# Prompt attention in a decoder layer: keys on the partitions, four heads at a time

## The chip, the cores and the metric

The kernel runs on one core of one Trainium2 chip. Its time is the device time of one execution in microseconds (us); three runs of the kernel before gave 2463.38, 2450.45 and 2455.8, median 2455.8. The profile is one more execution, recorded by the hardware profiler.

## The reference

One inference step of one decoder layer for a prompt of 1024 tokens and 8 sample sequences of 4 tokens (width 1024). A normalized input is projected to three mixers (sparse attention, a recurrent block, gated linear attention), whose outputs are merged and followed by an MLP. The change is in the sparse attention of the prompt, which has 8 heads of 64 in 2 groups (4 heads share a key/value head) and three branches for each head:

```python
# compressed: one key per 32 tokens; selected: all blocks here (16 of 16); window: the last 512 tokens
s = einsum(q, k) * 64 ** -0.5 + bias[bucket(pos_q - pos_k)]
s = where(mask, s, -inf)                     # causal; in the window also dist < 512
p = exp(s - max(s)) / max(sum(exp(s - max(s))), 1e-30)
o = g_cmp * (p_c @ v_c) + g_sel * (p_s @ v_s) + g_win * (p_w @ v_w)    # g: sigmoid gates per head
```

The bias depends on the distance alone and is constant from 128 tokens on; the constant part falls out of the softmax, so only the two nearest key tiles of 128 need a bias.

## The kernel before

All stages run one after the other; each is a block in which every engine has its own written-out program, and engines wait for each other by semaphores only. There is no planner: the order on an engine is the order of its program. Matrix products with weights are done as three f16 products (high by high, low by high, high by low parts); `Dense` (L360 to L434) streams weight tiles of 512 KB through four f32 buffers `w32`, and ScalarE and VectorE split each into f16 parts `wH` and `wL`. `load_ahead`, `split_hi_ahead` and `split_lo_ahead` (L374 to L385) start the next stage's weights in the stage before.

`project_nsa` (L618) makes queries, keys and values; GpSimd keeps the values as `vN` (L759, L760). `sample_attention` (L788) handles the sample tokens; on the side VectorE splits the prompt's keys into f16 parts: high parts `kH` twice, on both halves of the partitions (L972), low parts `kL` twice (L977).

`prompt_attention` (L1045 to L1310) follows. Queries of one head sit in `qP` with the high part on one half of the 128 partitions and the low part on the other, so one f16 matmul multiplies both with the high keys (L1139). A job is one query tile of 128 tokens (i = 0 to 7), one group g and one branch: compressed (4 to 32 keys), selected (tiles 0 to i) or window (at most 5 tiles). There are 48 jobs, and a loop over the four heads of a group, on every engine, runs through them: four passes. For each job:

- TensorE makes scores with 128 queries on the partitions and up to 1024 keys in the row (`score`, L1130), by `kH` and then `kL`.
- VectorE adds bias and window mask in place (L1225 to L1230) and takes the negated row maximum (L1233).
- ScalarE exponentiates with that maximum as bias and accumulates the row's sum (L1200).
- TensorE transposes each 128x128 tile of probabilities (f32, L1148), ScalarE copies it out of PSUM (L1183), and TensorE multiplies it by the values (f32, L1160), 128x64 per tile.
- VectorE makes factors of gate over sum (L1245 to L1248) and adds the branch to `oacc` (L1257, L1260).

TensorE's order in a pass is: scores of job j, values of job j - 4, transposes of job j - 2:

```python
for j in range(NJ + 4):
    if j < NJ:
        score(hh, j)
    if j >= 4:
        values(hh, j - 4)
    if 2 <= j < NJ + 2:
        turn(hh, j - 2)
```

The f16 parts of the queries are made in the first pass (L1107, L1110), most of them on GpSimd. A second block transposes `oacc` to `oH`/`oL` (L1286 to L1307), while SP loads the next stage's first weights and ScalarE and VectorE split the first of them (L380, L384).

## Time and profile before

| | us |
|---|---|
| median of three runs (lowest, highest) | 2455.8 (2450.45, 2463.38) |
| profiled execution: span from first to last instruction | 2447.7 |
| TensorE matmuls busy | 2199.6 (90%) |
| VectorE busy | 852.1 (35%) |
| ScalarE busy | 666.5 (27%) |
| GpSimd busy | 328.9 (13%) |
| mean granted TensorE clock | 0.915 |

The page gives no other time of the profiled execution than its span; 2455.8 is 8.1 above it. A busy share is an average over all stages. Matmuls are pipelined and the ends of their records are modelled, so records overlap and a TensorE that is "busy" may still be waiting between two matmuls. An f32 matmul leaves two records. The granted clock is 1.00 or 0.50 of 2.4 GHz at any moment; other values are means over a stretch.

### The profile page before, as it was taken

The numbers are of one execution on the slowest core, as the hardware profiler recorded it, in microseconds if no ns is written. First come the engines' busy times: TensorE is split into PE (matmuls) and PEld (weight loads), VectorE is DVE, ScalarE is ACT, GpSimd is POOL, SyncE is SP. The second block draws the span as 40 slices with busy tenths as digits, with TensorE's granted clock in tenths as the row PEclk, the third lists the DMA queues.
The fourth block names the chain that finished last, engine by engine and source line by source line (L and its number), as shares of the span: only waits on it lengthen the run. The fifth ranks groups of instructions, "written<-read, shape, count | busy, mean of one in ns | idle before, by whom it ended". The sixth has DMA issues, their size and how long they took to land. (4 is left out here: it accounts for less than half of the span.)

```text
span 2447.7 us, 38062 instructions
## 1 busy us (share of the span) xinstructions
PE 2199.6 (90%) x14280; PEld 1485.4 (61%) x14280; DVE 852.1 (35%) x1612; ACT 666.5 (27%) x1188; POOL 328.9 (13%) x245
## 2 busy tenths in 40 slices
PE   4889966799999884999699999987799999999998
PEld 2446633578778653666466666655466666666666
DVE  4211131667667536234322222223322222222223
ACT  5122221365465344332212221112211111111112
POOL 4200022300000001001100000000340330420410
PEclk7898978587698997999899999998899999999999
DMA  6421432000000302100321113021111111111111
GB/s 208 113 69 52 159 105 65 1 2 1 1 1 1 75 3 51 43 17 18 84 52 51 39 51 86 0 105 34 43 52 51 43 51 51 43 51 50 44 34 71
DMA packets 182794, 127.02 MB, mean 52 GB/s; under 512 B 8400, under 2 KB 175462, under 8 KB 182378
## 3 DMA queue, kind: packets, MB, share of 16 engines
q1 hardware_dynamic: 173258, 113.01, 15.8%
q0 software_dynamic: 4640, 10.60, 1.6%
q10 hardware_dynamic: 4800, 2.30, 0.3%
q8 instruction: 40, 0.66, 0.1%
q14 instruction: 56, 0.46, 0.1%
HBM read 111.68 MB, written 18.36 MB: 53 GB/s over the span
## 5 line engine op out<-in xcount | busy, mean ns | idle before, releaser
L426 PE MATMUL ps<-hH,wH 128*128 128x352 f16 x1536 | 318.3, 317 | 47.7 <-ACTq L399 27.8
L426 PE MATMUL ps<-hL,wH 128*128 128x352 f16 x1536 | 317.2, 316 | 0.0
L426 PE MATMUL ps<-hH,wL 128*128 128x352 f16 x1536 | 316.4, 315 | 0.0
L413 DVE SCALAR_TENSOR_TENSOR wL<-w,wH 128x1024 f16<-128x1024 f32 x98 | 120.1, 1225 | 322.0 <-ACT wH L406 307.7
L426 PEld LDWEIGHTS ps<-hH,wH 128*128 128x128 f16 x1536 | 151.3, 99 | 132.7 <-issue 48.3
L426 PE MATMUL ps<-mH,wH 128*128 128x352 f16 x960 | 196.2, 314 | 10.4 <-DVEq L399 8.1
L426 PEld LDWEIGHTS ps<-hL,wH 128*128 128x128 f16 x1536 | 151.9, 99 | 82.1
L426 PEld LDWEIGHTS ps<-hH,wL 128*128 128x128 f16 x1536 | 151.5, 99 | 81.2
L426 PE MATMUL ps<-mH,wL 128*128 128x352 f16 x960 | 196.0, 313 | 0.0
L426 PE MATMUL ps<-mL,wH 128*128 128x352 f16 x960 | 196.0, 313 | 0.0
L406 ACT ACTIVATE wH<-w 128x1024 f16<-128x1024 f32 x98 | 102.6, 1047 | 247.1 <-PE ps L426 225.4
L1160 PE MATMUL ps<-vN,oL 128*128 128x64 f32 x1056 | 162.4, 306 | 0.1
L1160 PEld LDWEIGHTS ps<-vN,oL 128*128 128x128 f32 x1056 | 154.0, 222 | 5.3 <-issue 3.3
L1183 ACT COPY oL<-ps 128x512 f32<-128x512 f32 (+7 forms) x256 | 96.8, 404 | 133.3 <-PE ps L1148 133.1
L426 PEld LDWEIGHTS ps<-mH,wH 128*128 128x128 f16 x960 | 93.9, 98 | 60.7 <-DVE wL L384 8.4
L2012 PE MATMUL ps<-hH,mgwH 128*128 128x352 f16 x576 | 118.2, 315 | 12.5 <-DVE mgwL L2059 12.5
L2229 DVE SCALAR_TENSOR_TENSOR xT<-ps,xT 128x1056 f32<-128x1056 f32 x32 | 40.3, 1258 | 245.0 <-PE ps L426 245.0
L426 PEld LDWEIGHTS ps<-mL,wH 128*128 128x128 f16 x960 | 94.0, 98 | 49.6
L426 PEld LDWEIGHTS ps<-mH,wL 128*128 128x128 f16 x960 | 94.0, 98 | 49.6
L2247 POOL TENSOR_TENSOR mpsq<-mprelu 128x1056 f32<-128x1056 f32 x32 | 62.3, 1946 | 445.4 <-DVE mprelu L2226 445.4
L1148 PE MATMUL ps<-cst,oL 128*128 128x128 f32 (+7 forms) x592 | 121.1, 321 | 0.0
L2012 PE MATMUL ps<-hL,mgwH 128*128 128x352 f16 x576 | 118.0, 314 | 0.0
(406 smaller groups left out, 2955.6 us busy)
## 6 DMA issues: line engine op xcount, KB each, us to landing
w<-in_mlp_w SPq DMA_DIRECT2D x64, 512.0 KB, 4.0
w<-in_w_in SPq DMA_DIRECT2D x32, 512.0 KB, 4.1
mgw<-in_w_in SPq DMA_DIRECT2D x24, 512.0 KB, 4.0
mgw<-in_w_branch SPq DMA_DIRECT2D x24, 256.0 KB, 4.3
xTd<-xT SPq DMA_DIRECT2D x1, 4224.0 KB, 12.3
xT<-xTd SPq DMA_DIRECT2D x1, 4224.0 KB, 14.0
xn<-in_x_prompt SPq DMA_DIRECT2D x8, 512.0 KB, 3.7
oH<-in_cache_nsa_cmp_kv SPq DMA_DIRECT2D x32, 128.0 KB, 3.0
```

The lines of the kernel that those rows point to most:

```text
L406: self.k.nc.scalar.activation(self.k.wH[:, slot % 2, :, :], self.k.w32[:, slot, :, :], ACT.Copy, scale=WS).then_inc(self.hi, 1)
L413: self.k.nc.vector.scalar_tensor_tensor(self.k.wL[:, slot % 2, :, :], self.k.w32[:, slot, :, :], WS, self.k.wH[:, slot % 2, :, :], ALU.mul ...
L426: ins = nc.tensor.matmul(k.ps[:, 3 * parity + c, 0:CH], w[:, kt, :], x[:, kt, c * CH:(c + 1) * CH], start=(kt == 0 and x is inH and w is w ...
L1148: ins = nc.tensor.transpose(k.ps[0:n, 4 + bank, u * P:(u + 1) * P], prob[:, j % 3, (a + u) * P:(a + u) * P + n], k.c('ident'))
L1160: ins = nc.tensor.matmul(k.ps[:, 6 + j % 2, 0:DH], probT[0:n, j % 3, u, :], v, start=(u == 0), stop=(u == len(tiles) - 1))
L1183: copy(probT[0:n, j % 3, a:a + len(tiles), :].rearrange("p u n -> p (u n)"), k.ps[0:n, 4 + bank, 0:w]).then_inc(out[bank], 1)
L2012: ins = nc.tensor.matmul(k.ps[:, c, 0:CH], w[:, s, kt, :], x[:, kt, c * CH:(c + 1) * CH], start=(kt == 0 and w is wH and x is k.hH), stop= ...
L2229: ins = nc.vector.scalar_tensor_tensor(cols3(xT[:, t - KD, :]), ps, 1 / WS, cols3(xT[:, t - KD, :]), ALU.mult, ALU.add)
L2247: nc.gpsimd.tensor_tensor(sq[:, :], relu[:, t % 2, :], relu[:, t % 2, :], ALU.mult).then_inc(squared, 1)
```

## The change

The prompt attention is rewritten in one block without a loop. `attention_order` lists 148 tiles: for each u (query tile i = u // 2, group g = u % 2) one compressed tile, i + 1 selected and up to 5 window tiles. One step, a slot, treats one tile for the four heads of a group at once, with 128 keys on the partitions and 4 x 128 queries in the row:

- TensorE multiplies high keys by `qP` (512 columns) and then low keys by `Q2`, the high queries again; a compressed tile has a third matmul with its bias. VectorE adds the bias or mask of a near tile (`toepT`, `winmaskT`) to the scores in place. ScalarE exponentiates without bias or sum. The result already has keys on the partitions, so it is the stationary operand of the value matmul as it is: there is no transpose and no copy. The values have a 65th column of ones (`vA`, `vc`), whose product is the sum.
- The row maxima are found ahead, with queries on the partitions as before but from the high keys alone, in 154 pieces of up to 512 columns (`bound`); bias and mask enter through f16 matmuls with 64 times the identity. VectorE takes the maxima (`part_max`, `mx`, `neg`); TensorE turns them into rows, ScalarE copies the rows into three unused partitions of `Q2`, and marks of 64 in the same rows of `kL` and `kcL` subtract them from the scores inside the matmul.
- VectorE divides by the sums, multiplies by the gates and writes the compressed branch to `oacc`, the others to `tmp`; GpSimd adds these. The final transposes, their copies and low parts run inside the same order, six and seven slots after a query tile's last.
- `load_ahead` waits for the last score, since the keys lie in `w32`; `Q2` of group 0 lies in the buffers of `wH` and `wL`. Queries of the first 256 tokens are split by ScalarE and VectorE, the others by GpSimd.
- Three constants are added (170 columns of 128 f32), the low parts of keys are made once instead of twice, and the values are kept in rows of 66.

The diff, cut to its core:

```diff
                ('headsum', 128), ('tokrow', 256), ('headhot', 24), ('seqcols', 256), ('seqrows', 8),
-               ('winmask_s', 4), ('blk', 16), ('bucket', 384)):
+               ('winmask_s', 4), ('blk', 16), ('bucket', 384), ('winmaskT', 128), ('mark', 6), ('esel', 36)):
...
@@ project_nsa: values kept by GpSimd @@
                     pool.wait_ge(first_out, t + 1)
                     pool.wait_ge(second_out, t + 1)
-                    nc.gpsimd.tensor_copy(k.vN[:, t, 0, :], nat[:, t % 3, 384:512])
-                    nc.gpsimd.tensor_copy(k.vN[:, t, 1, :], nat[:, t % 3, 640:768]).then_inc(vals_kept, 1)
+                    nc.gpsimd.tensor_copy(k.vA[:, t, 0, :, 0:DH], nat[:, t % 3, 384:512].rearrange("p (g n) -> p g n", g=G))
+                    nc.gpsimd.tensor_copy(k.vA[:, t, 1, :, 0:DH], nat[:, t % 3, 640:768].rearrange("p (g n) -> p g n", g=G)).then_inc(vals_kept, 1)
+                nc.gpsimd.memset(k.vA[:, :, :, :, DH:DH + 1], 1.0)
...
@@ sample_attention: low parts of the keys @@
             dve.wait_ge(s["khigh"], 8)
             for g in range(G):
-                for u in range(G):
-                    tt(k.kL[half[u], g], k.kT[half[g], :, 0:SEQ], k.kH[half[g], g], ALU.subtract)
-                    tt(k.kcL[half[u], g, :], k.kcT[half[g], 8, :], k.kcH[half[g], g, :], ALU.subtract)
+                tt(k.kL[half[g], g], k.kT[half[g], :, 0:SEQ], k.kH[half[g], g], ALU.subtract)
+                tt(k.kcL[half[g], g, :], k.kcT[half[g], 8, :], k.kcH[half[g], g, :], ALU.subtract)
+                mark = k.c('mark')[half[1 - g], g * 3:g * 3 + 3]
+                nc.vector.tensor_copy(k.kcL[half[1 - g], g, :], mark[:, 0:1].broadcast_to([DH, NCB]))
+                nc.vector.tensor_copy(k.kL[half[1 - g], g], mark[:, 1:3].unsqueeze(2).broadcast_to([DH, 2, SEQ]))
...
@@ the order, and prompt_attention @@
+def attention_order():
+    tiles, first, pieces = [], [], []
+    for u in range(2 * NT):
+        i = u // 2
+        first.append(len(tiles))
+        spans = ((0, 1), (0, i + 1), (max(0, i - WIN // P), i + 1))
+        for kind, (a, b) in enumerate(spans):
+            for t in range(a, b):
+                tiles.append((u, kind, t, t == a, t == b - 1))
+        pieces.append((u, 0, 0, 0, HPG, 0, 0))
+        for kind in (1, 2):
+            a, b = spans[kind]
+            for part, (t0, m) in enumerate(((a, min(4, b - a)), (a + 4, b - a - 4))):
+                for h in range(0, HPG if m > 0 else 0, 4 // max(m, 1)):
+                    pieces.append((u, kind, part, h, 4 // m, t0, m))
+    last = {p[0]: x for x, p in enumerate(pieces)}
+    slots = [min(first[v] - 6 - (last[v] - x) * 4 // 5 for v in range(p[0], 2 * NT)) for x, p in enumerate(pieces)]
+    return tiles, pieces, slots, last
...
+    tiles, pieces, slots, last_piece = attention_order()
+    N, NU = len(tiles), 2 * NT
+    S0, S1 = min(slots), len(tiles) + 9
+    in_slot = {s: [x for x in range(len(pieces)) if slots[x] == s] for s in range(S0, S1)}
+    rows_at = {slots[last_piece[u]] + 2: u for u in range(NU)}
+    run = [sum(t[3] for t in tiles[:n + 1]) - 1 for n in range(N)]
+    ends = [n for n in range(N) if tiles[n][4]]
+    combined_at = {n + 3: r for r, n in enumerate(ends)}
+    final_at = {ends[6 * i + 5] + 6: i for i in range(NT)}
+    adjusted = [0]
+    for u, kind, t, _, _ in tiles:
+        adjusted.append(adjusted[-1] + (kind > 0 and (t >= u // 2 - 1 or (kind == 2 and t == u // 2 - WIN // P))))
...
+    kH, kL, kcH, kcL, Q2, toepT = k.kH, k.kL, k.kcH, k.kcL, k.q2, k.toepT
+    qP = flat(k.oH[:, 4:12, :])[:, 0:H * SEQ].rearrange("p (h t) -> p h t", h=H)
+    spare = flat(k.oL[:, 4:12, :])
+    prob = spare[:, 0:4096].bitcast(F32).rearrange("p (u n) -> p u n", u=4)
+    toep16 = spare[:, 4096:6144].rearrange("p (h n) -> p h n", h=H)
+    biasC = spare[0:16, 6144:7168].rearrange("p (h n) -> p h n", h=H)
+    tmp = spare[:, 7168:8192].bitcast(F32).rearrange("p (u n) -> p u n", u=2)
...
+        @block.sync
+        def _(sp):
+            sp.wait_ge(scored, N)
+            nxt.load_ahead(sp)
...
+            for g in range(G):
+                nc.gpsimd.memset(Q2[g][half[1 - g], :, :], 0.0).then_inc(zeroed, 1)
+            for a, b in ((256, 512), (512, 1024)):
+                for g in range(G):
+                    q, hi, lo, again = split(g, a, b)
+                    settle(nc.gpsimd.tensor_copy(hi, q))
+                    settle(nc.gpsimd.tensor_tensor(lo, q, hi, ALU.subtract))
+                    settle(nc.gpsimd.tensor_copy(again, hi))
+                    pool.sem_inc(q_more, 1)
...
+            for u in range(NU):
+                for kind in (1, 2):
+                    r = 3 * u + kind
+                    pool.wait_ge(combined, r + 1)
+                    if kind == 2:
+                        pool.wait_ge(summed, 2 * u + 1)
+                    acc = oacc[:, u // 2, u % 2 * 256:u % 2 * 256 + 256]
+                    nc.gpsimd.tensor_tensor(acc, acc, tmp[:, kind - 1, :], ALU.add).then_inc(summed, 1)
+        @block.tensor
+        def _(pe):
+            for near in range(2):
+                for hg in range(G):
+                    for h in range(HPG):
+                        ins = nc.tensor.transpose(k.ps[:, 2 + 2 * near + hg, h * P:(h + 1) * P],
+                                                  k.toep[:, hg * HPG + h, near * P:(near + 1) * P], k.c('ident'))
+                    ins.then_inc(tables, 1)
+            pe.wait_ge(near_made, 1)
+            for h in range(H):
+                ins = nc.tensor.transpose(k.ps[0:16, 6 + h // 4, h % 4 * P:(h % 4 + 1) * P], near_hl[:, h, :], k.c('ident'))
+                if h % 4 == 3:
+                    ins.then_inc(tables, 1)
+            pe.wait_ge(consts_made, 1)
+            pe.wait_ge(q_high, 2)
+            pe.wait_ge(q_low, 4)
...
+            def bound(x):
+                u, kind, part, h0, nh, t0, m = pieces[x]
+                if x >= 2:
+                    pe.wait_ge(reduced, x - 1)
+                w = 4 * (i + 1) if kind == 0 else m * P
+                out = by_head(k.ps[:, BA + x % 2, 0:nh * w], nh)
+                near = min(2, i + 1)
+                for h in range(nh):
+                    kk = kcH[:, g, 0:w] if kind == 0 else kH[:, g, kind - 1, t0 * P:t0 * P + w]
+                    ins = nc.tensor.matmul(out[:, h, :], qP[:, g * HPG + h0 + h, cols(u)], kk, start=(h == 0),
+                                           stop=(h == nh - 1 and not windowed and not biased))
...
+                    if biased:
+                        ins = nc.tensor.matmul(out[:, :, (a - t0) * P:], ident64[:, :], bias[:, :, (a - i + 1) * P:(t0 + m - i + 1) * P], start=False, stop=True)
+                return ins
...
+            for s in range(S0, S1):
+                if 0 <= s < N:
+                    pe.wait_ge(rows_out, u + 1)
+                    if s >= 3:
+                        pe.wait_ge(exped, s - 2)
+                    out = k.ps[0:w, BS + s % 3, :]
+                    hi, lo = (kcH[:, g, 0:w], kcL[:, g, 0:w]) if kind == 0 else (kH[:, g, kind - 1, t * P:(t + 1) * P], kL[:, g, kind - 1, t * P:(t + 1) * P])
+                    nc.tensor.matmul(out, hi, qP[:, heads(u), cols(u)], start=True, stop=False)
+                    ins = nc.tensor.matmul(out, lo, Q2[g][:, :, cols(u)], start=False, stop=(kind > 0))
+                    if kind == 0:
+                        ins = nc.tensor.matmul(out, esel[:, 32 - 4 * i:36], biasC[:, heads(u), :], start=False, stop=True)
                     ins.then_inc(scored, 1)
...
+                    ins = bound(x)
+                    ins.then_inc(bounded, 1)
+                n = s - 2
+                if 0 <= n < N:
+                    pe.wait_ge(exped, n + 1)
+                    if first and r >= 2:
+                        pe.wait_ge(combined, r - 1)
+                    v = vc[0:w, g, 0:DH + 1] if kind == 0 else k.vA[:, t, kind - 1, g, 0:DH + 1]
+                    for h in range(HPG):
+                        ins = nc.tensor.matmul(k.ps[:, BO + r % 2, h * 66:h * 66 + DH + 1], prob[0:w, n % 4, h * P:(h + 1) * P], v,
+                                               start=(first and h == 0), stop=(last and h == HPG - 1))
+                    ins.then_inc(valued, 1)
+                if s in rows_at:
+                    u = rows_at[s]
+                    pe.wait_ge(negated, u + 1)
+                    pe.wait_ge(rows_out, u)
...
+                    b = base[u % 2]
+                    for h in range(HPG):
+                        ins = nc.tensor.matmul(k.ps[b:b + 3, BM, h * P:(h + 1) * P], neg[:, u, h, :], ident16[:, :], start=True, stop=True)
+                    ins.then_inc(rows, 1)
+                if s in final_at:
+                    i = final_at[s]
+                    pe.wait_ge(summed, 4 * i + 4)
+                    pe.wait_ge(rows_out, sum(x <= s for x in rows_at))
...
+                    for m in range(4):
+                        ins = nc.tensor.transpose(k.ps[:, BM, m * P:(m + 1) * P], oacc[:, i, m * P:(m + 1) * P], k.c('ident'))
+                    ins.then_inc(fin, 1)
...
+            act.wait_ge(zeroed, 2)
+            for s in range(S0, S1):
+                if 0 <= s < N:
+                    w = keys(s)
+                    if adjusted[s + 1] > adjusted[s]:
+                        act.wait_ge(adjust, adjusted[s + 1])
+                        act.wait_ge(scored, s + 1)
+                    if s >= 4:
+                        act.wait_ge(valued, s - 3)
+                    nc.scalar.activation(prob[0:w, s % 4, :], k.ps[0:w, BS + s % 3, :], ACT.Exp).then_inc(exped, 1)
+                if s in rows_at:
+                    u = rows_at[s]
+                    b = base[u % 2]
+                    act.wait_ge(rows, u + 1)
+                    nc.scalar.copy(Q2[u % 2][b:b + 3, :, cols(u)], by_head(k.ps[b:b + 3, BM, :])).then_inc(rows_out, 1)
+                if s in final_at:
+                    i = final_at[s]
+                    act.wait_ge(fin, i + 1)
+                    nc.scalar.copy(final(k.oH, i), by_head(k.ps[:, BM, :])).then_inc(fin_hi, 1)
+            nxt.split_hi_ahead(act)
...
+            ts(toep16, k.toep[:, :, :], 1 / MS, CLIP, ALU.mult, ALU.max)
+            ts(wmask16[:, :], k.c('winmask'), 1 / MS, CLIP, ALU.mult, ALU.max)
...
+            ts(ident64[:, :], k.c('ident'), MS, None, ALU.mult).then_inc(consts_made, 1)
+            for g in range(G):
+                q, hi, lo, again = split(g, 0, 256)
+                dve.wait_ge(q_high, g + 1)
+                tt(lo, q, hi, ALU.subtract).then_inc(q_low, 1)
+                nc.vector.tensor_copy(again, hi).then_inc(q_low, 1)
...
+            for s in range(S0, S1):
+                if 0 <= s < N and adjusted[s + 1] > adjusted[s]:
+                    u, kind, t, _, _ = tiles[s]
+                    near = t - (u // 2 - 1)
+                    more = toepT[:, heads(u), near, :] if near >= 0 else k.c('winmaskT').unsqueeze(1).broadcast_to([P, HPG, P])
+                    out = by_head(k.ps[:, BS + s % 3, :])
+                    dve.wait_ge(scored, s + 1)
+                    tt(out, out, more, ALU.add).then_inc(adjust, 1)
+                for x in in_slot[s]:
+                    u, kind, part, h0, nh, t0, m = pieces[x]
+                    w = 4 * (u // 2 + 1) if kind == 0 else m * P
+                    dve.wait_ge(bounded, x + 1)
+                    red(part_max[:, u % 2, h0:h0 + nh, kind, part], by_head(k.ps[:, BA + x % 2, 0:nh * w], nh), AX, ALU.max).then_inc(reduced, 1)
+                    if x == last_piece[u]:
+                        dve.wait_ge(reduced, x + 1)
+                        settle(red(mx[:, u % 2, :], part_max[:, u % 2].rearrange("p h k r -> p (h k) r"), AX, ALU.max))
+                        ts(neg[:, u].rearrange("p h k -> p (h k)"), mx[:, u % 2, :], -1 / MS, 1e6 / MS, ALU.mult, ALU.min).then_inc(negated, 1)
+                if s in combined_at:
+                    r = combined_at[s]
+                    u, kind = r // 3, r % 3
+                    dve.wait_ge(valued, ends[r] + 1)
+                    o = by_head(k.ps[:, BO + r % 2, 0:66 * HPG])
+                    f = fac[:, r % 4, :]
+                    settle(ts(f, o[:, :, DH], 1e-30, None, ALU.max))
+                    settle(nc.vector.reciprocal(f, f))
+                    z = kind * H + u % 2 * HPG
+                    settle(tt(f, f, k.gN[:, u // 2, z:z + HPG], ALU.mult))
+                    out = oacc[:, u // 2, u % 2 * 256:u % 2 * 256 + 256] if kind == 0 else tmp[:, kind - 1, :]
+                    if kind and u:
+                        dve.wait_ge(summed, 2 * (u - 1) + kind)
+                    tt(by_head(out), o[:, :, 0:DH], f.unsqueeze(2).broadcast_to([P, HPG, DH]), ALU.mult).then_inc(combined, 1)
+                if s - 1 in final_at:
+                    i = final_at[s - 1]
...
+                    tt(final(k.oL, i), by_head(k.ps[:, BM, :]), final(k.oH, i), ALU.subtract).then_inc(fin_lo, 1)
+            nxt.split_lo_ahead(dve)
...
@@ build: buffers @@
         k.oH, k.oL = sb("oH", [P, 12, T], F16), sb("oL", [P, 12, T], F16)
         k.w32 = sb("w32", [P, 4, KD, P])
-        k.wH, k.wL = sb("wH", [P, 2, KD, P], F16), sb("wL", [P, 2, KD, P], F16)
+        k.w16 = sb("w16", [P, 4, KD, P], F16)
+        k.wH, k.wL = k.w16[:, 0:2], k.w16[:, 2:4]
         k.ps = ctx.enter_context(nc.psum_tensor("ps", [P, 8, 512], F32))
...
+            k.vA = sb2("vA", [P, NT, 2, G, 66])
+            shared = sb2("vS_toepT", [P, H * 2 * P])
...
+            k.q2 = [x.rearrange("p (h t) -> p h t", h=HPG) for x in (k.w16[:, :, :, :].rearrange("p a b n -> p (a b n)"),
+                                                                     flat(k.cmpT[:, :, :]).bitcast(F16)[:, 0:HPG * SEQ])]
```

## Rows read from the trace of the kernel before

**Rows 1.** Timeline, stage start: start us, us, engine, line, [idle before <-releaser].

```profile
431.10 1.04 ACT L1107 CAST oH<-qT 64x1024 f16<-64x1024 f32 x1 [26.82 <-PEq L798]
...
431.85 1.22 DVE L1110 TENSOR_TENSOR oH<-qT,oH 64x1024 f16<-64x1024 f32 x1
...
435.12 2.12 POOL L1107 CAST oH<-qT 64x1024 f16<-64x1024 f32 x2
...
435.49 0.18 PE L1139 MATMUL ps<-kcH,oH 128*128 128x4 f16 x1 [6.18 <-POOL oH L1110]
...
443.90 4.31 POOL L1110 TENSOR_TENSOR oH<-qT,oH 64x1024 f16<-64x1024 f32 x2
...
444.28 1.76 DVE L1245 TENSOR_SCALAR pastat<-pastat 128x3 f32<-128x3 f32 x1
...
458.22 0.16 DVE L1245 TENSOR_SCALAR pastat<-pastat 128x3 f32<-128x3 f32 x1
```

**Rows 2.** Timeline, the end of the stage, SP and VectorE.

```profile
810.87 4.01 SPq L376 DMA_DIRECT2D w<-in_w_in  x4
...
817.20 1.23 DVE L384 SCALAR_TENSOR_TENSOR wL<-w,wH 128x1024 f16<-128x1024 f32 x1
```

**Rows 3.** Windows: length, busy us of PE, PEld, DVE, ACT, POOL; clock, DMA.

```profile
431.00:460.00 29.00, 15.08 (x68) 10.22 (x69) 22.73 (x56) 9.28 (x38) 21.72 (x13) 0.50 0.00 1
460.00:487.00 27.00, 27.00 (x117) 21.59 (x116) 15.46 (x54) 11.12 (x36) 0.00 (x0) 0.50 0.00 1
487.00:532.00 45.00, 44.98 (x365) 37.95 (x363) 33.55 (x107) 31.44 (x85) 0.00 (x0) 1.00 0.01 1
532.00:575.00 43.00, 38.16 (x184) 29.50 (x182) 25.27 (x98) 18.25 (x69) 0.00 (x0) 0.57 0.00 1
...
624.00:671.00 47.00, 42.29 (x201) 32.86 (x200) 26.95 (x106) 19.85 (x75) 0.00 (x0) 0.57 0.00 1
```

**Rows 4.** Windows of 6 us at the first turn of the loop.

```profile
532.00:538.00 6.00, 3.19 (x32) 3.02 (x30) 0.57 (x2) 0.75 (x2) 0.00 (x0) 1.00 0.01 4
538.00:544.00 6.00, 4.12 (x21) 2.67 (x21) 4.38 (x21) 3.18 (x16) 0.00 (x0) 0.50 0.01 3
```

**Rows 5.** Groups by line and form, 431 to 821 us: busy us, mean ns.

```profile
L1160 PE MATMUL ps<-vN,oL 128*128 128x64 f32 x1056 | 162.4, 306 | 0.1
...
L1148 PE MATMUL ps<-cst,oL 128*128 128x128 f32 x528 | 99.1, 318 | 0.0
...
L1230 DVE TENSOR_TENSOR ps<-ps,toep 128x256 f32<-128x256 f32 x112 | 48.1, 429 | 41.6 <-PE ps L1139 38.6 <-DVE pastat L1248 2.6
...
L1233 DVE TENSOR_REDUCE pastat<-ps 128x1 f32<-128x512 f32 x16 | 11.1, 692 | 0.6
L1200 ACT ACTIVATE oL<-ps,pastat 128x512 f32<-128x512 f32 x16 | 10.9, 683 | 0.0
```

**Rows 6.** Timeline of the weight loads, end of the third pass.

```profile
716.52 0.57 PEld L1148 LDWEIGHTS ps<-cst,oL 128*128 128x128 f32 x5
717.03 2.98 PEld L1160 LDWEIGHTS ps<-vN,oL 128*128 128x128 f32 x26
```

**Rows 7.** Timeline of TensorE in the next stage's projection.

```profile
825.21 0.61 PE L426 MATMUL ps<-hH,wL 128*128 128x352 f16 x3
825.66 0.61 PE L426 MATMUL ps<-hH,wH 128*128 128x352 f16 x3
```

**Rows 8.** Line 1427, VectorE: count, min/median/max ns, first and last start.

```profile
L1427 DVE TENSOR_SCALAR lrxc<-lrxin,vec x4: 812/814/815, 838.0 to 881.7; 128x1024 f32<-128x1024 f32 x4
```

**Rows 9.** Groups by line and form, GpSimd, 800 to 1000 us.

```profile
L1539 POOL MEMSET lrgw<- 128x1024 f32 x1 | 1.0, 951 | 364.2 <-POOLq L1274 364.2
```

**Rows 10.** Timeline of the kernel's start, TensorE.

```profile
7.03 4.50 PE L208 MATMUL ps<-cst,xn 128*128 128x128 f32 x20 [7.03 <-DMA xn<-in_x_prompt]
```

**Rows 11.** Timeline of VectorE in the sample attention.

```profile
337.08 0.18 DVE L990 COPY saxs<-ps 128x24 f32<-128x24 f32 x1 [11.24 <-PE ps L887]
```

More of the change, by code:

```diff
@@ L105, in shape_constants @@
     put('bucket', b)
+    put('winmaskT', np.where(i <= j, -BIG, 0.0))
+    mark = np.zeros((P, 6), np.float32)
+    for g in range(G):
+        for kind in range(3):
+            mark[(1 - g) * DH + kind, g * 3 + kind] = 64.0
+    put('mark', mark)
+    put('esel', 64.0 * (np.arange(16)[:, None] % 8 + 28 == np.arange(36)[None]))
     return c
@@ L1044, in prompt_attention @@
 def prompt_attention(k, nxt):
     nc, d = k.nc, k.d
-    C, S, W = range(3)
-    jobs = []
-    for i in range(NT):
-        for g in range(G):
-            for kind in (C, S, W):
-                first = {C: 0, S: 0, W: max(0, i - WIN // P)}[kind]
-                jobs.append((i, g, kind, [0] if kind == C else list(range(first, i + 1))))
-    NJ = len(jobs)
-    groups, count = [], [0, 0]
-    for i, g, kind, tiles in jobs:
-        mine = []
-        for a in range(0, len(tiles), 4):
-            bank = (count[0] + count[1]) % 2
-            mine.append((bank, count[bank], count[0] + count[1], tiles[a:a + 4], a))
-            count[bank] += 1
-        groups.append(mine)
@@ new lines, in prompt_attention @@
+    adjusted = [0]
+    for u, kind, t, _, _ in tiles:
+        adjusted.append(adjusted[-1] + (kind > 0 and (t >= u // 2 - 1 or (kind == 2 and t == u // 2 - WIN // P))))
+    half = [slice(g * DH, (g + 1) * DH) for g in range(G)]
+    base = (DH, 0)
+    BA, BS, BO, BM = 0, 2, 5, 7
+    MS = 64.0
+    CLIP = -60000.0
+    kH, kL, kcH, kcL, Q2, toepT = k.kH, k.kL, k.kcH, k.kcL, k.q2, k.toepT
+    qP = flat(k.oH[:, 4:12, :])[:, 0:H * SEQ].rearrange("p (h t) -> p h t", h=H)
+    spare = flat(k.oL[:, 4:12, :])
```

309 lines of the change are left out of this document (101 added, 208 removed).

## The prediction

> **What bounds the kernel now.** I read the windows of the attention stage first. It runs from 431.1 us (first copy of the queries [rows 1]) to 818.4 us (end of the weight split behind it [rows 2]): 387.3 us of a span of 2447.7. In the windows [rows 3] TensorE is busy almost throughout, so TensorE sets the end; but the reader is to look at the granted clock beside it. Each of the four passes of the head loop begins at 0.50, the 1.2 GHz level, and comes to 1.00 only in its second half: 56 us of the first pass, by the means of 0.57 about 37 and 40 us of the next two, and some 35 of the last. That is some 168 us at half clock, of which half, 84 us, is lost. What TensorE did before the fall stands in [rows 4]: it was busy for 3.19 of 6 us, at the turn of the loop. And having no idle time in the records is not enough to bring the clock back: 27.00 of 27 us busy at 0.50 [rows 3].
>
> Then the groups by line and form give what TensorE does here: 1056 records of 128x64 f32 values (two for one matmul) and 528 f32 transposes of 128x128, beside the f16 scores [rows 5]. At full clock 26 value records follow each other in 2.98 us, 0.1146 us each, and their weight loads fill that time [rows 6]; three f16 matmuls of 352 columns take 0.45 us, 0.149 each or 2.36 columns per ns [rows 7]. By these prices the stage before is 592 value matmuls (148 tiles of 128 keys x 4 heads) x 0.229 = 136, 592 transposes at 0.114 [rows 6] = 67, and 2 x 68,000 score columns = 58: 261 us. It took 380 before the tail; 119 went to the clock and to waits at the starts of the passes.
>
> **The change part by part.** I call one step of the new order (one tile of keys for four heads) a slot; there are 148, and the order gives 154 pieces of the maximum pass.
>
> TensorE, at full clock:
> - Scores: 148 tiles x 2 matmuls of 512 columns, and a third for the 16 compressed tiles: 312 x 0.217 [rows 7] = 67.7.
> - Maximum pass: 68,736 columns of q by high keys and 35,296 of bias and mask: 104,032 / 2.36 = 44.1. It is the half of the old scores that stays on the query side; the exact scores come on top.
> - Values: still 592 f32 matmuls with a 128x128 stationary operand. The column of ones makes 65 of 64 moving columns, but the weight load sets the pace [rows 6]: 135.7.
> - 592 transposes go (-67). Added: 64 row matmuls (0.06 each, 4), 32 final transposes, moved in from the old second block (4), and some 5 for pieces of one or two tiles, whose matmuls are short.
> - Three changes between kinds of matmul per slot. Ends: 0, and 0.1 where a weight load (0.114) stays uncovered; [rows 6] shows two kinds, at 716.52 and 717.03, without a gap between them, so I take 0.02: 9.
> - 11 pieces run ahead of slot 0 and are counted below: -4.
> Sum 265.5. So TensorE's work hardly changes (261 to 265). The gain can come only from the clock and the waits; that is the point on which the forecast hangs.
>
> VectorE: 68 adds of a 128x512 bias or mask to the scores in place, 0.43 for 256 columns [rows 5], so 0.70: 48. Maxima over 68,736 columns, 0.69 for 512 [rows 5]: 96. Forty-eight combinations (clamp, reciprocal, gate, multiply of 4x64), about 1.15 with the steps between: 55. Maxima of the parts and bounds 7, finals 8 x 0.68: 5. Sum 211 against 265, a cover of 80%. It is not even: for the first three query tiles (i = 0 to 2) I count 7, 10 and 14 per group of heads against TensorE's 6, 9 and 12.5, and an add, a maximum and a combination in one slot make 2.6 against a slot of 1.75. Queued behind VectorE's waits are the next maximum, for which TensorE's next piece waits (two banks), and the next add, for which ScalarE's exponential waits. Ends: 0 if slack of two slots absorbs it all, 40 if each of the 48 combinations costs its 0.85 excess. I take 13.
>
> ScalarE: 148 exponentials of 128x512 at 0.68 [rows 5], 101, with copies of rows and finals 115: hidden. The copies of turned probabilities go, but they were hidden too.
>
> Clock: between 0 and, if it stays low for as long as in the first pass (56 us), 28. The new order has no loop turn where it could fall again. I take 10.
>
> Start. Before, the first score came at 435.5 [rows 1]. Now TensorE turns 24 tables, while VectorE makes the small bias table, a 128x2048 tensor_scalar (0.81 for 1024 [rows 8], so 1.6), four constants (1.0) and two low parts (1.22 [rows 1] + 0.7 each): 8. GpSimd clears two 64x4096 buffers meanwhile; 1024 columns took 0.95 [rows 9], so 7.6 for both. Whether VectorE's table steps wait for a clearing no row shows: 0 to 7.6, and I take 3, since the nearest row, a GpSimd subtract, did hold a step of VectorE (0.75 to 1.76 us for three columns beside it, 0.16 without [rows 1]). Setup 11. The 11 pieces ahead of slot 0, at half clock, take about 0.9 each, and twice TensorE waits some 1.5 for the negated maxima: 13.
>
> By the Trainium skill (SBUF — State Buffer, "SBUF: two separate sides") VectorE and GpSimd share one pair of ports, which whoever starts first keeps for its whole instruction. The row with 1.76 us agrees. By that rule the clearings hold VectorE as well, and the sum would be 4.6 longer than mine; it speaks against GpSimd's share of this change, whose two subtracts of 64x2048 come while the first combinations run.
>
> GpSimd: splitting the rest of the queries takes (a cast of 1.06, a subtract of 2.16 [rows 1] and a copy like the cast) x 2 for 256 columns of four heads and twice that for 512, 26 us after the clearings; it ends near 465, and the first sum that VectorE waits for on GpSimd is due at slot 7, near 467. Cover is thin: 0 to 6; it is in the 13 of VectorE.
>
> Tail: combination 1.1, GpSimd's sum 0.5, transposes 0.5, copy 0.6, split 1.06, low part 1.23 [rows 2], with hand-overs 6. The old tail was 7.5 (810.9 to 818.4 [rows 2]). The four weight loads, which sat at that block's start, now wait for the last score; 4 us [rows 2] beside the last values and this tail. SP has nothing else queued there.
>
> Elsewhere: 87 KB more constants in the first load. TensorE's first transposes waited 7.03 us [rows 10] for loads behind it; a tenth of that, 0 to 0.7: I take 0.3. Two subtracts on keys become two copies; VectorE idled 11.24 us behind them [rows 11]: 0. The copies of values into the padded buffer are as many as before, and GpSimd waits for ScalarE there: 0.
>
> Sum: 11 + 13 + 265.5 + 10 + 13 + 6 = 318.5 against 387.3, so 68.8 less, 68.5 with the load. The profiled execution's span is 2447.7, and the median of the three runs 2455.8, 8.1 above; I take the gain off the median: **2387 us**. Its own range, from the ends of clock (0 to 28), VectorE (0 to 40) and start (-3 to 5) with not all at one end: 2362 to 2412.
>
> **Rivals.**
> - Better: the clock comes up in the prelude and VectorE hides. For it: TensorE's work has no more transposes and one long run of 148 slots. Then 11 + 13 + 265.5 + 6 = 295.5, 2364.
> - VectorE and the hand-over between engines pace the slots. For it: 80% busy with three engines in one chain per tile, as in the old starts of passes, where VectorE was busy 22.73 of 29 us and TensorE 15.08 [rows 3]. Against: two slots of slack. At 2.15 us per slot (1.43 mean VectorE work, 0.43 until the score is there, 0.3 of hand-overs): 318 + 24 + 10 + 6 = 358, 2427.
> - Slower: the clock does not come back. The place is the first slots; the price is TensorE's whole work at 1.2 GHz, 2 x 265.5 = 531, + 24 + 6 = 561, 2630. It decides if the low clock lasts past about 160 us, where 80 us lost eats the gain. For it: 27 us without idle time at 0.50 [rows 3]. Against: each pass came back by its second half, and the stretch from 487 to 532 us, with the same value matmuls, held 1.00 [rows 3].
>
> **How the numbers follow.** Forecast 0.55, better 0.20, VectorE-paced 0.19, slow clock 0.06. The range 2345 to 2430 leaves out the slow clock, the dearer half of the VectorE case and the tip of the better one, some 0.18. This kernel's runs spread by 0.5% (2450.45 to 2463.38), so about 0.5%, 12 us, is what counts as no change. Faster by more: forecast, better and three quarters of the paced case, 0.90; within: 0.04; slower: 0.06.
>
> **What would show it.** In the profile after: score at full clock 0.217 apart and values 0.115 per record; TensorE busy over 95% and the clock 1.00 from about 30 us into the stage; the stage 300 to 335 us long; VectorE at 60 to 70% of it; no stretch over 3 us without TensorE after slot 0. The prediction is wrong if TensorE shows waits on maxima or exponentials in most slots, or 0.50 beyond the first third, or if values of 65 columns cost more than 0.12 per record.

## The result, and the profile after

The changed kernel takes 2379.65 us (median of 4 runs, 2374.51 to 2382.62) against 2454.76 for the kernel before on the same chip: ratio 0.969, 95% interval 0.9662 to 0.9718, 75.1 us less. The forecast was 2387. The profiled execution has a span of 2372.7 us, 75.0 less than before, so its rows may be read for the whole.

The windows of the attention stage answer to [rows 3] and have their columns: setup (up to the first piece of the maximum pass), prelude (up to slot 0), then the slots in four parts, then the tail.

```profile
433.10:451.60 18.50, 4.53 (x25) 3.22 (x26) 18.27 (x14) 5.28 (x8) 17.47 (x8) 0.53 0.00 0
451.60:466.00 14.40, 9.36 (x56) 4.39 (x56) 11.45 (x17) 1.15 (x2) 13.84 (x6) 0.50 0.01 1
466.00:478.70 12.70, 11.85 (x81) 6.95 (x81) 10.77 (x28) 4.14 (x7) 4.00 (x5) 0.90 0.00 0
478.70:502.50 23.80, 23.80 (x98) 16.26 (x95) 12.73 (x39) 5.32 (x9) 2.90 (x4) 0.50 0.01 1
502.50:589.10 86.60, 85.38 (x650) 64.11 (x650) 63.45 (x161) 32.69 (x56) 8.72 (x12) 1.00 0.00 1
589.10:736.00 146.90, 146.82 (x1131) 116.16 (x1128) 90.09 (x210) 56.79 (x97) 10.19 (x14) 1.00 0.01 4
736.00:742.00 6.00, 1.12 (x5) 0.71 (x4) 2.84 (x6) 1.64 (x2) 0.72 (x1) 0.66 1.16 292
```

From the turned tables (433.1) to the end of the weight split (742.0) the stage takes 308.9 us, against 387.3 before. From 502.5 on TensorE is busy at 1.00, with 1.3 us of gaps up to the tail. Two stretches cost more than they must: 18.5 us of setup in which TensorE has 4.5 us of work and VectorE is "busy" throughout, and 23.8 us at 0.50 with TensorE never idle. The next stage's first projection comes 2.9 us after the stage's end as before; the stage starts 2.0 us later and what follows is 1.4 longer, so the stage's 78.4 become 75.0.

The setup in the timeline (start, length, engine, line), which answers to [rows 1]:

```profile
433.37 0.20 DVE L1333 CAST panc<-panc 128x64 f16<-128x64 f32 x1
433.60 3.57 DVE L1334 CAST panchl<-panc 128x64 f32<-128x64 f16 x1
433.60 3.51 POOL L1164 MEMSET w<- 64x4096 f16 x1 [22.12 <-POOLq L806]
...
437.16 4.51 POOL L1164 MEMSET cmpT<- 64x4096 f16 x1
...
438.15 3.61 DVE L1337 TENSOR_SCALAR pawm<-cst 128x128 f16<-128x128 f32 x1
...
451.58 0.24 PE L1213 MATMUL ps<-kcH,oH 128*128 128x4 f16 x4 [12.48 <-DVE cmpT L1345]
...
454.47 4.05 POOL L1169 TENSOR_TENSOR oH<-qT,oH 64x2048 f16<-64x2048 f32 x1
454.75 3.80 DVE L1366 TENSOR_SCALAR paneg<-pamx 128x12 f16<-128x12 f32 x1
...
458.61 0.58 PE L1273 MATMUL ps<-pai,paneg 128*3 128x128 f16 x4 [3.02 <-DVE paneg L1366]
```

Two casts of the same 128x64 elements, to f16 and back to f32: 0.20 us, and 3.57 beside a clearing of 3.51 (in e2, without it, 0.20 as well). VectorE's "18.27 us busy" is mostly that. TensorE waits 12.48 us for the queries that VectorE splits behind it. In the prelude the negation of 128x12 maxima takes 3.80 us beside a subtract of GpSimd's query split, and TensorE waits 3.02 us for it.

TensorE's timeline, first ahead of the fall of the clock, then a group of values behind a piece of the maximum pass, then near the end, where a slot is two scores and the values alone. This answers to [rows 6]:

```profile
475.33 1.08 PE L1260 MATMUL ps<-vA,oL 128*128 128x65 f32 x8 [0.52 <-DVE paoacc L1380]
...
477.44 1.07 PE L1260 MATMUL ps<-pavc,oL 4*128 4x65 f32 x8 [0.33 <-DVE oL L1380]
...
614.43 0.22 PE L1222 MATMUL ps<-oL,pai 128*128 128x128 f16 x1
614.49 1.06 PE L1260 MATMUL ps<-vA,oL 128*128 128x65 f32 x8
615.38 0.38 PE L1237 MATMUL ps<-oH,w 128*128 128x512 f16 x1
...
725.17 0.38 PE L1237 MATMUL ps<-oH,w 128*128 128x512 f16 x1
725.39 0.38 PE L1238 MATMUL ps<-cmpT,w 128*128 128x512 f16 x1
725.60 1.00 PE L1260 MATMUL ps<-vA,oL 128*128 128x65 f32 x8
726.44 0.38 PE L1237 MATMUL ps<-oH,w 128*128 128x512 f16 x1
...
733.22 2.79 PE L1260 MATMUL ps<-vA,oL 128*128 128x65 f32 x24
```

The first two rows are the only waits for VectorE between 474 and the fall at 478.7. At full clock a score starts 0.21 to 0.22 us after the one before; four value matmuls (8 records) take 0.84 until the next score, 0.105 per record, where 24 in a row take (2.79 - 1.00) / 16 = 0.112 each, close to the 0.1146 before. Behind a piece's bias they mostly take 0.89 (614.49 to 615.38); the mean of the 134 groups of eight records after 502.5 is 0.89. VectorE's groups came out as priced; line, form, count, busy us and mean ns:

```profile
L1362 DVE TENSOR_REDUCE papm<-ps 128x1 f32<-128x512 f32 x88 | 59.4, 685 | 25.6 <-PE ps L1222 18.5 <-PE ps L1213 6.8
...
L1357 DVE TENSOR_TENSOR ps<-ps,vS_toepT 128x512 f32<-128x512 f32 x60 | 41.8, 696 | 28.5 <-PE ps L1238 28.2
```

### The profile page after: what moved, and what is told of

The parts are those of the page before. It is cut to its first block and busy times, and to the rows that moved or that the text cites. A ratio compares the mean times of both kernels' runs of the same rounds, so it can differ in the third digit from the quotient of the medians.

```text
span 2372.7 us, 34450 instructions
## 1 busy us (share of the span) xinstructions
PE 2128.3 (90%) x13994; PEld 1410.8 (59%) x13994; DVE 795.3 (34%) x1207; ACT 561.0 (24%) x718; POOL 366.2 (15%) x281
## 5 line engine op out<-in xcount | busy, mean ns | idle before, releaser
L433 PE MATMUL ps<-hH,w 128*128 128x352 f16 x3072 | 552.4, 316 | 47.7 <-ACTq L406 27.8
L433 PEld LDWEIGHTS ps<-hH,w 128*128 128x128 f16 x3072 | 302.8, 99 | 213.6 <-issue 48.2
L433 PE MATMUL ps<-mH,w 128*128 128x352 f16 x1920 | 341.0, 313 | 8.8 <-DVEq L406 8.1
L433 PE MATMUL ps<-hL,w 128*128 128x352 f16 x1536 | 317.1, 316 | 0.0
L433 PEld LDWEIGHTS ps<-mH,w 128*128 128x128 f16 x1920 | 188.1, 98 | 108.5 <-DVE w L391 8.4
L420 DVE SCALAR_TENSOR_TENSOR w<-w 128x1024 f16<-128x1024 f32 x98 | 120.2, 1226 | 321.1 <-ACT w L413 308.0
L433 PEld LDWEIGHTS ps<-hL,w 128*128 128x128 f16 x1536 | 151.9, 99 | 81.9
L433 PE MATMUL ps<-mL,w 128*128 128x352 f16 x960 | 196.1, 313 | 0.0
L1260 PEld LDWEIGHTS ps<-vA,oL 128*128 128x128 f32 x1056 | 138.0, 198 | 13.7 <-issue 2.9
L1260 PE MATMUL ps<-vA,oL 128*128 128x65 f32 x1056 | 139.2, 277 | 1.0 <-DVE paoacc L1380 0.5
```

Of the source, the lines that this page charges most:

```text
L420: self.k.nc.vector.scalar_tensor_tensor(self.k.wL[:, slot % 2, :, :], self.k.w32[:, slot, :, :], WS, self.k.wH[:, slot % 2, :, :], ALU.mul ...
L433: ins = nc.tensor.matmul(k.ps[:, 3 * parity + c, 0:CH], w[:, kt, :], x[:, kt, c * CH:(c + 1) * CH], start=(kt == 0 and x is inH and w is w ...
L1260: ins = nc.tensor.matmul(k.ps[:, BO + r % 2, h * 66:h * 66 + DH + 1], prob[0:w, n % 4, h * P:(h + 1) * P], v, start=(first and h == 0), st ...
```

## The experiments

Single totals move by up to 1.5% (before: 2424.87 to 2462.09 in 13 runs on one chip) with stages that no experiment touches (in some the attention begins about 10 us later, at 441 to 444 us instead of 431 to 435), so stage parts are compared in the traces. "Main" is the run of slots, from the first score to the end of the last value matmul: 270.0 in the changed kernel.

**e1: the two clearings moved out of the stage.**

```diff
 # sample_attention, GpSimd, after its last load
+for g in range(G): nc.gpsimd.memset(k.q2[g][other half, :, :], 0.0)
 # prompt_attention, GpSimd
-    nc.gpsimd.memset(Q2[g][half[1 - g], :, :], 0.0).then_inc(zeroed, 1)
```

> GpSimd's two clearings of Q2 are moved into the sample attention, where GpSimd and VectorE stand idle; the split of the queries on GpSimd stays. Theory (a GpSimd instruction holds VectorE's next one for its whole length): in the changed kernel VectorE's setup steps stood from 433.6 to 437.2 and from 438.2 to 441.7 us beside the two clearings (3.51 and 4.51 us); without them the first piece of the maximum pass comes 10 to 12 us after the stage's start instead of 18.5, and the time is 2370 to 2374 against 2379.65. Rival (the steps wait for the turned tables or for the copies, the clearings only lie beside them): first piece still at 17 to 19 us, time within 2 us of 2380.

Measured: 2368.54 us (4 runs); first piece 14.6 us after the first table, neither 10 to 12 nor 18.5. The trace:

```profile
445.68 3.12 POOL L1170 TENSOR_TENSOR oH<-qT,oH 64x1024 f16<-64x1024 f32 x1
446.74 2.15 DVE L1337 TENSOR_SCALAR pawm<-cst 128x128 f16<-128x128 f32 x1
```

The query split on GpSimd moved up into the clearings' place and holds VectorE in turn. Main was 260.0 at 1.00: the second stretch at half clock did not come in this execution. So in the traces 4 us of e1's gain are setup, and 10 are main, which the edit does not touch.

**e2: the query split moved as well.** ScalarE and VectorE make all parts of the queries in the sample attention's last 25 us, where both were idle.

```diff
 # sample_attention, ScalarE, at its end (and the copies into Q2 behind it)
+act.wait_ge(s["score"], NB)
+nc.scalar.copy(hi, q).then_inc(s["qhi"], 1)
 # sample_attention, VectorE, ahead of its last wait
+dve.wait_ge(s["qhi"], g + 1); tt(lo, q, hi, ALU.subtract)
 # prompt_attention: the splits on all three engines and their waits go
```

> As e1, and the whole query split too is moved into the sample attention's last 25 us, where ScalarE (26.8 us idle) makes the high parts and their copies and VectorE (26.2 us idle) the low parts; GpSimd does nothing in the setup. Theory: first piece within 5 to 8 us of the stage's start, slot 0 within 15 to 18 instead of 32.9, so 15 to 18 us less: 2362 to 2365; if the second stretch at half clock (478 to 502 us) is a consequence of that start, 12 less again, 2350 to 2353. Rival: the prelude is bound by TensorE at half clock and the maxima, and slot 0 comes at 24 us or later: 2371 or more; the added steps lengthen the sample attention's end by up to 3.

Measured: 2349.37 us (4 runs, 2343.76 to 2357.23), ratio to the kernel before 0.9604 (0.9535 to 0.9674), with e12 the best complete version here. VectorE's setup and the windows of prelude and main:

```profile
432.58 0.20 DVE L1338 CAST panc<-panc 128x64 f16<-128x64 f32 x1
432.81 0.20 DVE L1339 CAST panchl<-panc 128x64 f32<-128x64 f16 x1
```

```profile
437.50:444.75 7.25, 6.07 (x56) 3.14 (x54) 5.50 (x14) 1.73 (x3) 0.00 (x0) 0.94 0.00 0
444.75:557.80 113.05, 109.34 (x824) 80.22 (x824) 85.44 (x227) 42.16 (x72) 12.31 (x17) 1.00 0.00 1
557.80:704.70 146.90, 146.82 (x1131) 116.17 (x1129) 90.15 (x210) 56.79 (x97) 10.16 (x14) 1.00 0.01 3
```

The cast that took 3.57 us takes 0.20; setup and prelude shrink from 32.9 to 12.4 us, main to 260.0 at 1.00. The stage begins at 432.3, so the added steps did not show in the sample attention. The theory's first step holds. Its second, that the later stretch at half clock follows from the slow start, is not shown: e12 has the same start and fell.

**e5: less work for VectorE.**

```diff
-if 0 <= s < N and adjusted[s + 1] > adjusted[s]:      # the 68 additions
+if False:
-red(part_max[...], by_head(k.ps[...]), AX, ALU.max)
+red(part_max[...], by_head(k.ps[...])[:, :, 0:w // 2], AX, ALU.max)
```

> The changed kernel with VectorE's work cut from some 210 to 115 us: the 68 additions of bias and mask to the scores are left out, and every maximum is taken over the first half of its columns; TensorE's work is the same. Theory (TensorE sets the end from about 30 us into the stage, VectorE is hidden): within 0 to 6 us of 2379.65, and, if the gaps of 0.5 and 0.3 us behind combinations near 475 to 477 us brought the second fall of the clock, 10 to 12 less, 2362 to 2370. Rival (VectorE and the hand-overs still pace part of the slots): the main run of slots shortens by 13 or more at an unchanged clock, 2350 to 2366.

The lines of ScalarE that wait for the additions go too. Measured: 2360.7 us (4 runs), main 256.9 without the second fall of the clock. Its two parts stand against 113.05 and 146.90 of e2:

```profile
474.20:585.00 110.80, 109.53 (x824) 80.49 (x824) 54.13 (x193) 42.20 (x72) 15.61 (x21) 0.99 0.00 1
585.00:731.10 146.10, 146.10 (x1131) 116.14 (x1128) 51.47 (x174) 57.28 (x97) 10.15 (x14) 1.00 0.01 3
```

VectorE does 105.6 us of work in main instead of 175.6, 70 less (the expectation had 95). They are worth 3.1 us, at most 1.1 more for the 0.99 of the first part, and most of that in the first 60 slots. VectorE is hidden. (e5 keeps the query split on GpSimd, but so does e1, whose main is that of e2.)

**e6 and e7: TensorE's two prices, on e2.** e6 leaves out the score by the low keys; e7 moves 33 columns per value matmul.

```diff
-ins = nc.tensor.matmul(out, lo, Q2[g][:, :, cols(u)], start=False, stop=(kind > 0))   # e6
-v = ... k.vA[:, t, kind - 1, g, 0:DH + 1]                                              # e7
+v = ... k.vA[:, t, kind - 1, g, 32:DH + 1]
```

> e2 without the score matmuls by the low parts of the keys (148 of 512 columns), which also leaves the maxima unsubtracted. Theory (TensorE's work sets the end after slot 0): 148 x 0.215 = 32 less, the main run of slots 228 to 231 instead of 260. Rival (VectorE, some 205 us of work in that stretch, and the hand-overs take over as soon as TensorE is shorter): 238 to 250.

> e2 with 33 moving columns in each value matmul in place of 65 (the last 32 value columns and the ones; VectorE writes these 32 twice). Theory (the f32 weight load of 128x128 sets the pace): still 0.84 us for four, main run 260 within 2. Rival (the moving columns set the pace, which the change raised from 64 to 65): about half, 0.42 to 0.5 us for four, main run 200 to 215, or paced by VectorE at 230.

Measured, one run each: e6 2321.9 us, main 241.9; e7 2349.78 us, main 257.8. e6's windows, the first 60 slots and the other 88, as those of e2 above; and e7's TensorE:

```profile
444.50:556.80 112.30, 107.72 (x763) 82.95 (x763) 85.04 (x227) 41.68 (x72) 12.31 (x17) 0.89 0.00 1
556.80:686.40 129.60, 128.42 (x1043) 108.05 (x1042) 89.70 (x211) 56.23 (x97) 10.15 (x14) 1.00 0.02 4
```

```profile
698.34 0.98 PE L1269 MATMUL ps<-vA,oL 128*128 128x33 f32 x8
699.15 0.38 PE L1248 MATMUL ps<-oH,w 128*128 128x512 f16 x1
```

e6's main is 18 us shorter than e2's 260.0, where the theory had 29 to 32 and the rival 10 to 22: by that number the rival's. But the clock was 0.89 in e6's first 60 slots. In the other 88 both run at 1.00, and e6 takes 129.60 where e2 takes 146.90: 17.3 us, 0.197 for each score left out, which is 29 for 148. The work came off, as the theory had it, and in the first slots the clock took it back. e7: half the columns, 0.81 instead of 0.84. So the moving columns do not set the pace of the values, and the column of ones costs nothing; what is left are the weight loads, which filled that time in [rows 6].

**e4 and e9: the kernel before with the clock held up** by extra matmuls at the turns of the loop, three in a step and one.

```diff
+if j < 9 or j >= NJ:
+    for _ in range(FILL):                      # 3 in e4, 1 in e9
+        nc.tensor.matmul(k.ps[:, 1, :], kH[:, 0, 0, 0:P], kH[:, 0, 0, 0:512], start=True, stop=True)
```

> The kernel before, with three extra f16 matmuls of 512 columns in each of the last 4 and the first 9 steps of every pass, into a PSUM bank that nothing reads there: 39 per pass, 156 in all, 34 us at full clock if nothing hides them. Theory (the gain came from the clock, which fell at each turn of the loop after TensorE had stood idle for 2 to 3 of 6 us): the clock stays at 1.00 through most of passes 2 to 4; each pass gains some 20 us and pays 4 to 8, so 2400 to 2425 against 2455. Rival (the starts of the passes are slow by their waits and by VectorE, and the clock only follows): the falls stay, 2455 to 2475.

> The kernel before with one extra f16 matmul of 512 columns (three in e4) in each of the last 4 and first 9 steps of a pass: 13 per pass, 2.8 us at full clock. Theory (the clock alone was worth some 20 us a pass): if the mean clock of passes 2 to 4 rises from 0.80 to 0.94 or more as in e4 (88 us a pass with 8.5 us of extra matmuls), a pass takes 72 to 76. Rival (at full clock the waits at the start of a pass, VectorE's chain, take the place of the slow clock): 80 to 86 at that clock. If one matmul a step does not hold the clock, 91 to 93, and nothing follows.

Measured: e4 2453.82 us (10 runs), ratio 1.0028 (0.999 to 1.0066), no change; e9 2455.52 (one run). Windows by pass of the loop: passes 1, 2 and 4 of the kernel before, pass 2 of e4, and passes 2 and 4 of e9.

```profile
435.50:534.90 99.40, 89.96 (x574) 72.64 (x575) 70.10 (x215) 51.55 (x160) 18.52 (x12) 0.74 0.01 1
534.90:626.60 91.70, 86.85 (x576) 70.61 (x575) 61.89 (x216) 51.48 (x160) 0.00 (x0) 0.80 0.00 1
...
720.00:810.90 90.90, 85.32 (x574) 69.07 (x574) 62.06 (x217) 51.58 (x160) 0.00 (x0) 0.81 0.00 1
```

```profile
534.60:623.00 88.40, 83.32 (x613) 64.34 (x612) 61.11 (x216) 52.06 (x160) 0.00 (x0) 0.96 0.00 1
```

```profile
546.00:636.20 90.20, 86.59 (x587) 69.00 (x586) 61.59 (x217) 51.62 (x160) 0.00 (x0) 0.83 0.00 1
731.20:817.00 85.80, 79.10 (x587) 62.83 (x586) 61.24 (x217) 51.88 (x160) 0.00 (x0) 0.94 0.00 1
```

In e4 the clock did stay up (0.96 in pass 2), and the pass still took 88.4. The four passes together were 6 us shorter (369 of 375), too little to show in the totals. In e9 one matmul a step held the clock in pass 4 alone: 85.8 us at 0.94, in the rival's 80 to 86 and not the theory's 72 to 76. At full clock that would be some 85.8 - 0.06 x 85.8 = 80.7, less at most 2.8 of extra work: 78, where TensorE's own work by the prices of before is 261 / 4 = 65. So the estimate, from one pass of one run, is that at full clock a pass takes 13 to 16 us beyond that work. Of these 6.7 are gaps in TensorE's records (85.80 - 79.10); the rest are waits that the modelled ends hide, or matmuls dearer than their price. The clock alone was worth some 11 to 14 us of a pass, not 20, and in e4 the 8.5 us of extra matmuls ate most of it.

**e8 and e10: two changes of kind per slot, on e2.**

```diff
 high score of slot s
+first two value matmuls of slot s - 2
 low score of slot s
 pieces of the maximum pass
-four value matmuls
+last two value matmuls               # e10: VectorE's combination ahead of the slot's maxima
```

> e2 with TensorE's order changed inside a slot: high score matmul, two value matmuls, low score matmul, pieces of the maximum pass, the other two value matmuls; nothing else moves. Theory (a change from f16 to f32 values hides half of one f32 weight load: four value matmuls take 0.84 us between scores, 8 records x 0.112 = 0.90 in a run of 24): a second change per slot saves another 0.05 to 0.06, so a slot without a piece takes 1.21 instead of 1.27, the main run of slots 250 to 254 instead of 260, the time 2338 to 2344 against 2349. Rival (the saving is the overlap at the end of the group only, and each change costs as much again): 1.27 to 1.33 per slot, main 260 to 269.

> e8 with VectorE's combination put ahead of the maxima of the same slot. In e8 a slot without a piece took 1.21 us as its theory had it, but the first value matmuls of a branch, now half a slot earlier, waited up to 1.6 us for combinations, and the clock fell several times: main run 302 instead of 260. Theory (those waits brought the falls): without them the clock holds and the price of the slot comes through, main run 250 to 258, time 2338 to 2348. Rival (the interleaved order itself leaves less slack, or the falls have another cause): 275 to 305, time 2360 or more.

Measured: e8 2384.21 us (4 runs), main 302.4; e10 2361.17 (4 runs), main 284.1. TensorE in e8, the first value matmuls of a branch early in main, and a slot late in it:

```profile
451.11 0.38 PE L1266 MATMUL ps<-oH,w 128*128 128x512 f16 x1
453.11 0.63 PE L1249 MATMUL ps<-vA,oL 128*128 128x65 f32 x4 [1.62 <-DVE paoacc L1388]
...
692.53 0.38 PE L1266 MATMUL ps<-oH,w 128*128 128x512 f16 x1
692.74 0.56 PE L1249 MATMUL ps<-vA,oL 128*128 128x65 f32 x4
693.13 0.38 PE L1268 MATMUL ps<-cmpT,w 128*128 128x512 f16 x1
693.35 0.56 PE L1249 MATMUL ps<-vA,oL 128*128 128x65 f32 x4
693.74 0.38 PE L1266 MATMUL ps<-oH,w 128*128 128x512 f16 x1
```

In a slot without a piece the price is the theory's: 692.53 to 693.74, 1.21 us instead of 1.27. The time is not: values asked for half a slot earlier wait for VectorE's combination (1.62 us), and the clock falls. e10 shortens those waits and still falls. Its two parts:

```profile
443.70:582.20 138.50, 131.75 (x824) 97.18 (x824) 87.00 (x227) 42.08 (x72) 12.28 (x17) 0.84 0.00 1
582.20:727.80 145.60, 145.46 (x1130) 120.23 (x1128) 91.26 (x210) 56.43 (x98) 10.12 (x14) 1.00 0.01 4
```

The second part, at 1.00, gains 1.3 us over e2's 146.90, so of the 0.06 of a slot little comes through where most slots have pieces. The first loses 25, by the mean clock up to 0.16 x 138.5 = 22 of it to the clock. The theory that those waits alone brought the falls is not borne out.

**e11 and e12: the changed kernel again, and e2 with the combination first.**

> The changed kernel itself once more, beside the next two on one chip: whether the fall of the clock at 478 us and the return at 502 are there again. If it belongs to this order of waits: again 0.50 for some 23 us from 10 to 15 us after slot 0, main run of slots 268 to 272, time 2372 to 2385. If it is chance: main run 259 to 262 at 1.00.

> e2 with VectorE's combination of a branch put ahead of the maxima of the same slot. Theory (after slot 0 only short waits on combinations are left, 1.8 us in the trace of e2, and the gaps without a named wait): main run of slots 256 to 260 against 260.0. Rival (the maxima, now later, hold the next pieces of the maximum pass, for which TensorE has two banks): 260 to 268, and with a new fall of the clock up to 280.

Measured: e11 2376.82 us (4 runs, 2367.01 to 2383.64), main 265.0; e12 2350.45 (4 runs), main 271.2 in the profiled execution. e11's windows from slot 0, then e12's first part:

```profile
465.10:479.50 14.40, 12.89 (x92) 7.75 (x92) 11.71 (x30) 5.30 (x9) 4.76 (x6) 0.99 0.00 0
479.50:500.00 20.50, 19.54 (x108) 13.42 (x107) 13.75 (x43) 5.33 (x9) 2.17 (x3) 0.75 0.01 2
```

```profile
446.10:571.20 125.10, 121.75 (x824) 88.21 (x824) 86.70 (x227) 42.23 (x72) 12.31 (x17) 0.89 0.00 1
```

e11 falls again, later and for a shorter time: its main is 5 us above the 260.0 of e1 and e2, that of the first trace 10. That lies between the two expectations. So the fall comes in these first slots, and its length differs between executions. e12 has the start of e2 and fell nevertheless (main 11 us longer); its median is e2's. Nor do the waits that the profile names decide it: in the first 60 slots they sum to 1.3 us in the changed kernel and 2.5 in e12, which fell, and to 2.9 in e1 and e2, which did not. Each fall, and each time that none came, was seen in one execution. What decides whether the clock falls in the first 60 slots stays open. Apart from e8, no trace shows it falling in main after those.

## Why the prediction was right, step by step

The total was 7 us off, but two terms were 8 to 10 us too dear and one 7.5 too cheap. That they nearly cancel is luck; the place of the gain is not.

| step | forecast | measured |
|---|---|---|
| setup | 11 | 18.5 |
| prelude | 13 | 14.4 |
| TensorE, at full clock | 265.5 | 257 |
| half clock after slot 0 | 10 | 10 |
| VectorE and bursts | 13 | about 3 |
| tail | 6 | 6.0 |
| stage | 318.5 | 308.9 |

Measured for the clock is what main took beyond that of e1 and e2, where it held 1.00: 270.0 - 260.0. The windows' clock would give 0.5 x 23.8 + 0.1 x 12.7 = 13, 3 more, so not all time at half clock was lost here either. For TensorE it is what is left of 260.0 without the 3 for VectorE (e5).

- **Right: where the gain could come from.** TensorE's work hardly changed (261 by the prices of before, 257 measured), the transposes' 67 us were spent on the second score and the maximum pass, and the stage gained 78 all the same. e6 shows that TensorE's work sets the end, e5 that VectorE doesn't: the slack absorbs nearly all of it. The rival of a VectorE-paced run of slots and that of a clock that stays low both fall; the better one had VectorE right and the clock wrong.
- **Wrong in part: the split of the 119 us.** "Some 168 us at half clock, of which half, 84 us, is lost" counted waits twice: at full clock TensorE would have waited for some of that time. By the estimate from e9, 52 to 63 us of the 114 that four passes of before (375.4) took above 261 would have stayed at full clock, so the clock was about the other half. The change won both. Which of its parts took the waits away (no turn of the loop, four heads at once, maxima found ahead) was argued and not tested one by one. Holding the clock up in the old loop by extra matmuls won nothing in the total (e4).
- **Setup, mis-sized.** For the clearings I took 3 of 0 to 7.6 and counted GpSimd's split only for when it ends. The rows show VectorE's casts, copies and subtracts held for the length of whole GpSimd instructions, 3.57 us for a cast of 0.20. e2 has 5.2 us of setup where the change takes 18.5; of the 13.3 between them, 3.8 by the forecast's prices are VectorE's own two low parts and copies, which e2 makes earlier, and the rest is time held. The Trainium skill (SBUF — State Buffer, "SBUF: two separate sides") gives the rule: VectorE and GpSimd share one pair of ports, and whichever starts first, an instruction of GpSimd or one of VectorE that runs in a mode with two ports (or has two inputs in SBUF while GpSimd reads there), keeps the pair to its end. The trace agrees: the held cast ended at 437.17, the clearing at 437.11. I had weighed it at 4.6 us more for the clearings alone. e1 shows that the split does the same in their place, and the wait of 3.02 us in the prelude, where I had 1.5, came from the split as well.
- **Changes of kind, mis-sized the other way.** I priced four value matmuls at 8 x 0.1146 = 0.917 us and added 0.02 for each of three changes per slot, 9 us. The rows show no such loss: from its start to the next matmul's a group takes 0.84 us between scores and 0.89 on average, which makes the values 132 us instead of 135.7. With the 9 that is 13 too dear where the whole term was 8.5, so its other matmuls came some 4 dearer than priced; the runs don't part those further. e7 shows that it is not the moving columns that set the pace of the values.
- **Clock, right in size, wrong in place.** It did not stay low for long after the start; it rose between 468 and 470 us, fell at 478.7, after waits of 0.52 and 0.33 us for combinations, and came back at 502.5. I had put 1.00 from 30 us into the stage; it was 69. The 10 us were meant for a slow start, and I had argued that no place was left where the clock could fall again. It did, so the size came out by luck.
- **VectorE, mis-sized.** I took 13 of 0 to 40 for it; e5 shows about 3. Its work was near the forecast. One product in it is off: 68,736 columns at 0.69 us per 512 make 93 us, not 96. And the lower end of the forecast's own range, 2362, has all its three terms at their ends, against what it says; neither moves the result.
- **The rest.** "No stretch over 3 us without TensorE after slot 0" holds up to the tail. VectorE's share was 209.6 of 308.9 us, 68%, as forecast. The 0.3 us for the constants can't be told: the stage began 2.0 us later than before in one execution and 10 to 13 us later in executions of e1, e5 and e7, and nothing here tells what share is theirs.

## What to carry to other kernels

Time at half clock is not all lost time: before counting on the clock, ask what the engine would wait for at full clock. A mean clock read off a window gives the most that it can have cost. Setup work on GpSimd is not free beside VectorE even when no semaphore joins them; put it where VectorE is idle (e2: setup and prelude 20 us shorter by moving work that was already there). A busy share of VectorE in a setup says nothing until one instruction's length is held against its length elsewhere.

## What the runs showed that I had not expected

- A 128x64 cast on VectorE took 0.20 us alone and 3.57 beside GpSimd's clearing; the second clearing, 4.51 against 3.51 for the first, waited for VectorE in turn.
- The granted clock fell to 0.50 in main with TensorE 93% busy just before, and stayed there for 23.8 us of TensorE without idle time; the same kernel lost 10 us to this in one execution and 5 in another.
- Four f32 value matmuls between two f16 scores take 0.84 us with 65 columns and 0.81 with 33; two by two between scores, 0.39 each pair, 0.78 for four. Behind the short matmuls of a piece most of that gain is gone: 0.89.
